# Three output tiles side by side at a boundary, squares of the operand summed tile by tile on TensorE, and forget gates taken through ScalarE by function

## The reference, cut to what matters

```python
def rmsnorm(x, g):
    xf = x.astype(jnp.float32)
    y = xf * lax.rsqrt(jnp.mean(xf * xf, axis=-1, keepdims=True) + NORM_EPS)
    return y.astype(x.dtype) * g
# in the even mixer
z = h @ w_in
u, q, fz, i, g = jnp.split(z, cuts, axis=-1)
fz32 = jnp.clip(fz.astype(jnp.float32), -GATE_CLIP, GATE_CLIP)
logf = jax.nn.log_sigmoid(fz32) + jnp.log1p(lb * jnp.exp(-fz32))
k = (1.0 - lb) * jax.nn.sigmoid(-fz32)
# one layer of the first block
for l in range(DEPTH):
    y = even_mixer(h, ...) if l % 2 == 0 else odd_mixer(h, ...)    # h = rmsnorm(x, g[0])
    x = x + rmsnorm(y, g[1])
    h = rmsnorm(x, g[2])
    x = x + rmsnorm(memory_cross_attention(h, mem_n, ...), g[3])
    h = rmsnorm(x, g[4])
    x = x + rmsnorm(squared_relu_mlp(h, w_ff1[l], w_ff2[l]), g[5])
```

## Time and profile before

| | us |
|---|---|
| median of 3 runs (4279.80 to 4284.48) | 4281.89 |
| the profiled execution | 4284.98 |
| its span | 4283.7 |
| PE busy in it | 3712.3 (87%) |
| DVE, POOL, ACT busy | 2117.4, 1538.7, 1436.9 |
| mean granted clock of PE | 0.928 of 2.4 GHz |

### The profile page before, as it was taken

The page is one execution under the profiler, slowest core; times in us unless marked ns, Lnnn a source line. Parts: engine busy times, 40 slices in busy tenths (PEclk is TensorE's granted clock), DMA queues, the critical chain, the costliest instruction groups (busy, mean ns, idle before and its releaser), DMA issues.

```text
span 4283.7 us, 49996 instructions
## 1 busy us (share of the span) xinstructions
PE 3712.3 (87%) x19246; PEld 2975.4 (69%) x19246; DVE 2117.4 (49%) x4517; ACT 1436.9 (34%) x2089; POOL 1538.7 (36%) x738
## 2 busy tenths in 40 slices
PE   4966888998977888997747779788999999999998
PEld 4855656886934667885626648677887888888885
DVE  2037336655065346324776334999994333332324
ACT  3355333224233333233224332223443232323222
POOL 4722322443401324441732114232224444445452
PEclk8987999999978999998868899899999999999999
DMA  4510213442300213331200013334555444444442
GB/s 148 171 59 1 99 44 104 142 143 92 107 26 24 88 49 123 124 100 56 69 24 2 31 40 105 111 106 143 189 195 185 138 161 143 152 153 147 151 144 69
DMA packets 298044, 445.40 MB, mean 104 GB/s; under 512 B 8144, under 2 KB 219088, under 8 KB 295760
## 3 DMA queue, kind: packets, MB, share of 16 engines
q1 hardware_dynamic: 278640, 371.22, 26.5%
q0 software_dynamic: 19168, 70.98, 5.1%
HBM read 383.45 MB, written 58.72 MB: 103 GB/s over the span
## 4 chain that ended last, share of the span: by engine, by line
PE 71%; DVE 16%; issue 5%; ACT 4%; POOL 3%; DMA 1%; DVEq 0%; ACTq 0%; SPq 0%; POOLq 0%
PE bank L435 20%; PE bank L436 20%; PE bank L437 20%; PE bank L2412 3%; PE bank L511 2%; POOL split_low L421 2%; PE bank L1543 2%; PE bank L1777 1%; DVE arena_rw L2092 1%; POOL arena_rw L2290 1%; PE bank L1230 1%; DVE arena L2493 1%; DVE arena L2495 1%; DVE arena L2499 1%; DVE arena L2497 1%
## 5 line engine op out<-in xcount | busy, mean ns | idle before, releaser
L421 POOL TENSOR_TENSOR split_low<-weights,split_high 128x1024 fp32r<-128x1024 f32 x554 | 1336.1, 2419 | 2168.2 <-ACT split_high L413 2167.7
L435 PE MATMUL bank<-normed_high,split_high 128*128 128x512 f32 x2544 | 1017.3, 400 | 162.4 <-POOL split_low L421 75.3
L436 PE MATMUL bank<-normed_low,split_high 128*128 128x512 f32 x2544 | 1005.2, 395 | 0.0
L437 PE MATMUL bank<-normed_high,split_low 128*128 128x512 f32 x2544 | 1004.0, 395 | 0.0
L413 ACT CAST split_high<-weights 128x1024 fp32r<-128x1024 f32 x554 | 574.3, 1047 | 791.0 <-PE bank L437 694.4
L435 PEld LDWEIGHTS bank<-normed_high,split_high 128*128 128x128 f32 x2544 | 488.0, 192 | 279.3 <-issue 127.4
L435 PE MATMUL bank<-hidden_high,split_high 128*128 128x512 f32 x1536 | 600.9, 391 | 7.5 <-ACT hidden_high L2488 4.8
L437 PE MATMUL bank<-hidden_high,split_low 128*128 128x512 f32 x1536 | 599.2, 390 | 0.0
L436 PE MATMUL bank<-hidden_low,split_high 128*128 128x512 f32 x1536 | 599.0, 390 | 0.0
L437 PEld LDWEIGHTS bank<-normed_high,split_low 128*128 128x128 f32 x2544 | 486.7, 191 | 104.0
L436 PEld LDWEIGHTS bank<-normed_low,split_high 128*128 128x128 f32 x2544 | 488.0, 192 | 100.9 <-issue 1.2
(11 more groups left out here) (374 smaller groups left out, 4223.2 us busy)
## 6 DMA issues: line engine op xcount, KB each, us to landing
weights<-in_w_ff SPq DMA_DIRECT2D x64, 1024.0 KB, 5.4
weights<-in_peer_u SPq DMA_DIRECT2D x64, 1024.0 KB, 6.1
weights<-in_peer_v SPq DMA_DIRECT2D x64, 1024.0 KB, 5.0
gate_table<-arena SPq DMA_DIRECT2D x16, 2048.0 KB, 7.7
gates<-gate_table POOLq DMA_DIRECT2D x32, 1024.0 KB, 9.7
weights<-in_cond_w SPq DMA_DIRECT2D x24, 1024.0 KB, 5.2
early_table<-branch SPq DMA_DIRECT2D x72, 256.0 KB, 2.2
lates<-early_table POOLq DMA_DIRECT2D x18, 1024.0 KB, 11.0
```

Source lines behind the costliest of these rows:

```text
L421: pool.do.tensor_tensor(lo, raw_unit(u), hi.bitcast(F32), ALU.subtract).then_inc(*pool.sig("split_low", u))
L435: pe.do.matmul(o, ah, bh, start=first, stop=False)
L436: pe.do.matmul(o, ah, bl, start=False, stop=False)
L437: return pe.do.matmul(o, al, bh, start=False, stop=last)
```

## The change

1. `FIRST = 3`: `pe_first` grows three output tiles side by side in place of four, at all its places. The fourth is made by `pe_product(..., skip=FIRST)` after it.
2. At `mem0`, `mlp0`, `odd`, `mem1` and `mlp1` DVE's seven additions of squares are gone. PE multiplies each tile's square by the constant matrix within `pe_first`, behind the three triples of that tile, and adds the eight results in PSUM. `act_root` now waits for the last of them; ACT splits three units first (one in the MLPs).
3. The memory keys lose `pe_first`: the first output tile is made alone, then the sum, then the others; ACT splits three units before the root.
4. The forget gates: ACT does Sigmoid and Abs with each tile of f, and the four pairs of Exp and four pairs of Ln among the value copies. Their inputs and results lie in `y` and `e_b`, not in the small rings. DVE clips all four tiles first and makes the decay at the end.

```diff
+FIRST = 3
-        def pe_first(stage, ids, rhs, ready, emptied, width_out=T):
+        def pe_first(stage, ids, rhs, ready, emptied, square=None):
             for a in range(CT):
                 pe.wait_ge(ready(a))
-                for c in range(4):
+                for c in range(FIRST):
...
+                if square:
+                    pe_sum(stage[0], T, a, CT, mean, square(a), at("operand_square", stage[0], a), [("root_log", stage[0])])
...
-            if stage:
-                dve_operand_sum(stage, lambda c: y[:, c, :])
...
-                    pe_first(st, W["keys", l][0:2], mem_tile, ready, emptied, M)
+                    rest = pe_product(st, W["keys", l], mem_tile, ready, emptied, M)
+                    next(rest)
                     pe_operand_sum("mem", mem_square[:, 0, :], M)
-                    run(pe_product(st, W["keys", l][2:], mem_tile, ready, emptied, M, c_all=4))
+                    run(rest)
...
+            act_split(2 * W["keys", 0][0] + FIRST + AHEAD)
             act_root("mem", 0, NORM_EPS, mem_root, M)
...
             for c in range(4):
                 act_split(2 * W["E", "f"][0] + c + AHEAD)
-                f = dve_tmp.tile("clipped", c)
                 act.wait_ge(at("clipped", c))
-                act.do.activation(e_k[:, c, :], f, ACT.Sigmoid, scale=-1.0).then_inc(*act.sig("key_sigmoid", c))
...
+                act.do.activation(e_k[:, c, :], gate_in[c], ACT.Sigmoid, scale=-1.0).then_inc(*act.sig("key_sigmoid", c))
+                act.do.activation(e_b[:, c, :], gate_in[c], ACT.Abs).then_inc(*act.sig("gate_abs", c))
+            decays = act_decay()
             for n, i in enumerate(W["E", "i"]):
                 for tk in range(TT):
...
+                    next(decays)
+                    next(decays)
...
-            pe_first((st, "q"), ids[0:2], h_tile, h_ready(st), scaled_out((st, "q")))
-            rest = pe_product((st, "q"), ids[2:], h_tile, h_ready(st), scaled_out((st, "q")), c_all=4)
-            next(rest)
-            pe_operand_sum(st, y[:, 0, :])
+            pe_first((st, "q"), ids, h_tile, h_ready(st), scaled_out((st, "q")), squares)
+            rest = pe_product((st, "q"), ids, h_tile, h_ready(st), scaled_out((st, "q")), T, FIRST)
             run(rest)
...
-            act_split(2 * W["M", l, "q"][0] + 4)
-            act_root(st, 0, NORM_EPS, root)
+            act_split(2 * W["M", l, "q"][0] + FIRST + AHEAD)
+            act_root(st, CT - 1, NORM_EPS, root)
```

More of the change, by code:

```diff
@@ L469, in pe_first @@
                         pe.wait_ge(empty, split_ready(u))
-                    last = triple(banks.tile("product", stage, c)[:, 0:width_out],
+                    last = triple(banks.tile("product", stage, c),
                                   [w_[:, a, cols] for w_ in unit_tiles(u)], rhs(a), a == 0, a == CT - 1)
@@ L825, in build @@
         rec_state = [arena(2 * T + j * P, P) for j in range(2)]
+        gate_in, bound = [[y[:, 4 * j + c, :] for c in range(4)] for j in range(2)]
         N_LV = len(REC_LEVELS) + 1
@@ L966, in act_even, with act_decay @@
             act_close(EM, W["E", "o"])
+        def act_decay():
+            for c in range(4):
+                act.wait_ge(at("gate_abs", c))
+                act.do.activation(e_b[:, c, :], e_b[:, c, :], ACT.Exp, scale=-1.0).then_inc(*act.sig("gate_exp", c))
+                yield
+                act.do.activation(bound[c], gate_in[c], ACT.Exp, scale=-1.0).then_inc(*act.sig("bound_exp", c))
+                yield
+            act.wait_ge(at("lb_ready"))
+            for c in range(4):
+                act.wait_ge(at("gate_exp", c))
+                act.do.activation(e_b[:, c, :], e_b[:, c, :], ACT.Ln, bias=one).then_inc(*act.sig("soft", c))
+                yield
+                act.wait_ge(at("bound_exp", c))
+                act.do.activation(bound[c], bound[c], ACT.Ln, scale=lb[:, c:c + 1], bias=one
+                                  ).then_inc(*act.sig("bounded", c))
+                yield
         def rec_done(hd):
@@ L1017, in dve_even @@
             for c in range(4):
-                f, empty = dve_tmp.take("clipped", c)
-                dve.wait_ge(empty)
+                f = gate_in[c]
                 dve_scaled((EM, "f"), [c], lambda c: f)
@@ L1025, in dve_even @@
                                      ).then_inc(*dve.sig("rec_key", c))
-                e = act_tmp.tile("soft", c)
+            for c in range(4):
+                e = e_b[:, c, :]
                 dve.wait_ge(at("soft", c))
-                dve.do.scalar_tensor_tensor(out=e, in0=f, scalar=0.0, in1=e, op0=ALU.min, op1=ALU.subtract
+                dve.do.scalar_tensor_tensor(out=e, in0=gate_in[c], scalar=0.0, in1=e, op0=ALU.min, op1=ALU.subtract
                                             ).then_inc(*dve.sig("dve_step"))
                 dve.wait_ge(dve.last, at("bounded", c))
-                dve.do.tensor_tensor(e, e, act_tmp.tile("bounded", c), ALU.add).then_inc(*dve.sig("decay_step", c))
-                dve_tmp.give(("clipped", c), ("decay_step", c), ("bounded", c))
+                dve.do.tensor_tensor(e, e, bound[c], ALU.add).then_inc(*dve.sig("decay_step", c))
                 dve.wait_ge(dve.last, at("keep_tile_landed"))
-                dve.do.tensor_tensor_scan(out=e_b[:, c, :], data0=keep_tile, data1=e, initial=0.0,
+                dve.do.tensor_tensor_scan(out=e, data0=keep_tile, data1=e, initial=0.0,
                                           op0=ALU.mult, op1=ALU.add).then_inc(*dve.sig("decay_sum", c))
@@ L1423, in act_mlp @@
             end = mlp_end(l)
-            act_split(2 * W["F", l, "up", 0][0] + 4)
-            act_root(st, 0, NORM_EPS, root)
+            act_split(2 * W["F", l, "up", 0][0] + FIRST + 1)
+            act_root(st, CT - 1, NORM_EPS, root)
             for g in range(FF_GROUPS):
@@ L1496, in pe_odd @@
             ids = W["O", "q"]
-            pe_first((OM, "q"), ids[0:2], h_tile, ready, scaled_out((OM, "q")))
-            rest = pe_product((OM, "q"), ids[2:], h_tile, ready, scaled_out((OM, "q")), c_all=4)
-            next(rest)
-            pe_operand_sum(OM, y[:, 0, :])
+            pe_first((OM, "q"), ids, h_tile, ready, scaled_out((OM, "q")), squares)
+            rest = pe_product((OM, "q"), ids, h_tile, ready, scaled_out((OM, "q")), T, FIRST)
             run(rest)
@@ L1548, in act_odd @@
         def act_odd():
-            act_split(2 * W["O", "q"][0] + 4)
-            act_root(OM, 0, NORM_EPS, root)
+            act_split(2 * W["O", "q"][0] + FIRST + AHEAD)
+            act_root(OM, CT - 1, NORM_EPS, root)
             for c in range(2 * CT):
```

33 lines of the change are left out of this document (13 added, 20 removed).

## The result

Six executions of the changed kernel took 4234.58 to 4246.34 us, median **4241.91**; six of the kernel before had a median of 4284.80. The ratio is 0.989, 95% interval [0.9869, 0.9911]. The change saves 43 us, and the forecast was 64: faster, as forecast, but outside of 4208 to 4232.

What follows compares the result with a forecast made beforehand. PE's work and its waits were taken as the bound (71% of the chain is PE). Gains of 29.8 + 11.7 + 13.6 + 3.8 + 5.0 = 63.9 us gave 4221.1, less 3.1 for the median: 4218 us, range 4208 to 4232.

Steps and rivals of the forecast that it cites:

- Gates: Forget gates: splits no longer late, PE reaches g at 256.5 in place of 286.29, 29.8 us gained.
- Attention boundaries: `mem0`, `odd`, `mem1`: waits and slow restart go, seven more sums are paid; 3.9 us each, 11.7 in all.
- MLP boundaries: `mlp0`, `mlp1`: the sum ends with `pe_first`, so root and DVE's chain come 6.8 us earlier each, 13.6 in all.
- Second block: Its two `pe_first` lose the wait for the fifth unit, 1.9 us each with the drain, 3.8 in all.
- Keys: Memory keys: POOL's low parts come earlier, token root at 62.7 to 66 against 67.71; 5 us, bounds 1 and 8.
- The sum: All gains added over the whole kernel: 29.8 + 11.7 + 13.6 + 3.8 + 5.0 = 63.9 us.
- (d): PE stays at the low clock level all through `pe_first` at five boundaries, 97 us added: 4315 us; chance 0.02.
- (a): The 40 sums in TensorE cost 0.5 us more each, 20 us in all: 4238 us; chance 0.09.
- (b): Gates: ACT or DVE's decay chain becomes the bound in the values, g starts 10 us later: 4228 us; chance 0.08.
- (e): Nothing happens, because the time returns in a later wait such as for weights: 4280 us; chance 0.01.

Runs made afterwards that it cites:

- fillers: The changed kernel with two extra full-size products in PE's wait for DVE's sum in each scan round: median 4227.29 us, in a repeat 4222.51.
- the mixed version: The changed kernel with two extra products per scan round, DVE adding the attention boundaries' squares and TensorE the MLPs': median 4210.95 us, ratio 0.9791.
- the filled start: The changed kernel with three extra full-size products in PE's 1.03 us wait ahead of the first scan product: median 4242.24 us, profiled execution 4227.6.

## Why the prediction missed, by its own steps

- **Gates, 29.8.** Measured 35.5 - 5.8 = 29.7 at the first g product, and 31 us in the kernel that has this part alone. PE has no wait from f to g, and the values take 250.79 - 227.76 = 23.0, as said. Right.
- **Attention boundaries, 3.9 each.** Measured in the first profile 3.5 (`mem0`), 4.3 (`odd`) and 4.8 (`mem1`). Rounds of 2.95 us against 2.90, the stage 52.75 against 52.4. Right in size, and the working already had the reason: 8.2 of waits and 1.7 of slow restart gone, less 6.0 for seven more sums. What I didn't ask is what the part would give without those 6.0. With DVE's sums it gives 5 to 9.
- **MLP boundaries, 6.8 each.** 7.3 and 5.1. The root's Ln came 26.8 us behind the first triple, 25.5 forecast. In `mlp0` that is 5.5 us earlier than before and not 6.8; the missing part was made good by luck, since DVE's chain behind the root was 1.8 us shorter (from its first relu to its last modulation, 629.54 to 658.92 against 676.07 to 707.28).
- **Second block, 1.9 each.** 0.8 and 1.0, half of it: from the first product of the stage to its 192nd 46.20 us against 47.04 in `pe_rw`, and 46.18 against 47.15 in `pe_peer`. The waits of 1.73 us for the fifth unit are gone, but the products at the start took about 1 us longer at a lower granted clock (0.90 against 0.94 over the first 29.4 us of `pe_rw`).
- **Keys, 5.** 5.8; PE's fifth-tile wait went from 14.80 to 5.71.

```profile
48.19 0.55 PE L436 MATMUL bank<-mem_high,split_high 128*128 128x256 f32 x1 [5.71 <-POOL split_low L422]
```

- **The sum** to the scan's start is 58.9 against a forecast of 62 at that point, 3 us short, within the terms' own bounds.
- **The step that failed** is the one that isn't there. The sum took all work behind the last edit to keep its length, and the prediction costed the clock only as rival (d), in `pe_first`, where it stayed high but for the first rounds. It fell in the scan, some 370 us behind the nearest edited place (the `pe_first` of `pe_rw`, at 1951.67), and costs 18.5 us in the profiles. By the times this comes in nearly all executions of the changed kernel and in a third of those of before. Without the fall the changed kernel took 4224 (one execution) and 4222 to 4227 (medians with fillers), within the range that I gave though still above the forecast; before without it took 4285. The range had no case for it, and the rows to suspect it were there: a stretch of 64x64 products with a wait in each round. The executions of before that were shown ahead of the prediction, 4279.8 to 4284.5, had none above 4290, so they gave no warning.
- **The rivals.** (a), sums costlier by 0.5 us, would have given 4238, near the result, and was wrong: they cost what was said. A time that agrees with a rival proves nothing until its rows are looked at. (b), (d) and (e) did not come.

## What to carry to other kernels

When a change moves a long program in time, compare the granted clock of every stretch of both profiles, not only of those edited: here a stretch of small products with short waits lost its clock though none of its own instructions had changed, and four products ahead of it cost 21 us. Put idle-time products of full size into such waits; here two per round cost nothing and kept 18.5 us. And take an edit that does two things apart: adding the squares in TensorE paid where the root was waited for and cost where PE was the bound, and with the fillers in both the mixed version is 11.6 us faster than the change as made.

## What the runs showed of the hardware

- The granted clock of TensorE in a stretch does not depend on its own instructions alone: with 0.9 us of work ahead of the scan its 776 products ran at 0.52 in the profile, against 1.00 in that of before, and the kernel's median went from 4285.95 to 4306.67 us.
- At 1.2 GHz the scan's products filled nine tenths of PE's time (30.78 of 34.42 us), and the clock still stayed there for 51 us; it rose where products of 128x512 followed.
- Two executions of the same instructions can differ by 15 us over the first block: the point in `mlp1` that the first profile of the changed kernel passed at 1617.83 us, the profile with the filled start passed at 1602.63. Most of it is the granted clock again. Between the same two splits of ACT the first profile has 481.59 to 658.19 us at 0.93 and the other 480.24 to 650.72 at 0.98; between two later ones 1318.06 to 1625.46 at 0.95 against 1311.40 to 1610.27 at 0.97. The two stretches make 14.6 us of the difference. What decides it stays open.
